# Second mixer of a three-block network: the dense jobs' first piece of work goes into the scan, one gated group per job, centring on ScalarE

## Chip, cores and metric

One core of a Trainium2 chip runs the whole program: three network blocks, one after the other, in float32, at batch 1, 512 tokens and a width of 1024. The metric is the device time of one execution in microseconds. The kernel before took 3704.06 us, the median of three runs (3701.74 to 3704.71).

## What is computed

The change touches the mixer of the second block alone (`second_block` in the reference):

```python
xn = rmsnorm_2(h, mix_norm_w[l])
g_a, g_b, za, z, xbc, dt_raw = jnp.split(xn @ w_in[l], splits, axis=-1)
y_a = gmlp_mixer(za, ...) @ w_proj_a[l]
y_b = mamba2_mixer(z, xbc, dt_raw, ...) @ w_proj_b[l]
merged = sigmoid(g_a + gate_bias[l, 0]) * y_a + sigmoid(g_b + gate_bias[l, 1]) * y_b
h = h + merged @ w_out[l]
# gmlp_mixer: u, v = split(gelu(za)); v in 8 groups of 128 features
v = (vf - mu) * rsqrt(var + EPS_2) * ln_w + ln_b       # per token and group
sv = einsum('gts,bnsgd->bntgd', where(mask, w_s, 0), v) + b_s
return u * sv                                           # per group: "gating"
# mamba2_mixer: conv and silu on xbc, a chunked scan over 32 heads, then
y = (scan + d_skip * xs) * silu(z)                      # 2048 channels
y = yg * rsqrt(mean(yg * yg) + EPS_2) * norm_w          # yg: 4 groups of 512
```

## The kernel before

Each engine has its own program and waits on semaphores for the others; the order on each engine is written out by hand (`tensor`, `scalar`, `vector`, `gpsimd`, `sync` of `SecondMixer`). Activations lie as tiles of 128 channels by 512 tokens. In order of time the second mixer does the following.

**The scan.** 16 pairs of heads. For pair j TensorE turns the channel tile (`turn_pe`, L2375), VectorE makes two scaled copies of it (`factors_dve`, L2815), TensorE forms the chunk states (`states_pe`, L2384), VectorE carries them along (`state_dve`, L2822 and L2827), and TensorE adds up the pair's outputs (`outputs_pe`, L2398 and L2402), which VectorE adds to the skip term (L2683). The weights of the outputs come by another way: SyncE spreads a line of decays over the partitions (L2182) once the outputs of pair j-2 are done, GpSimd subtracts (`relative_pool`, L2483), ScalarE takes two exponentials (`decays_act`, L2602 and L2603), GpSimd (L2493) and VectorE (`aged_dve`, L2838) multiply.

**Tiles between the pairs.** So that TensorE is not idle in the scan, `side_until` lets it work through 30 more tiles of the input projection between those steps: 14 for the scan's own channels, which VectorE convolves (`convolve_dve`, L2797 and L2800) and ScalarE opens (`silu_act`, L2585), and 16 for the gMLP, which ScalarE evicts (`gelu_act`, L2594). A tile is 8 matmuls of 512 columns (weight 2 each, L2229) or 16 of 256 columns (weight 1, L2220), so `TILE` = 16. Each pair has three slots of `SHARE` = 11, after its turn, its states and its outputs. `slot_ends` tells ScalarE and VectorE after which slot they take up which tile. The tiles need 480 of 3 x 16 x 11 = 528, so they end in the slot behind the states of pair 14, and the last four slots are empty.

**The dense jobs.** Then come 28 jobs, each a Strassen step of 28 matmuls of 256 columns per pair of output tiles and 1024 inputs (`Sevens`, L998; the seven products are named 1 to 7 and run in the order 1, 2, 6, 5, 7, 3, 4, four matmuls each). Products 1; 2 and 6; 5 and 7; 3 and 4 share a bank each, so four banks hold a job. GpSimd makes three sums of the weights per slot beforehand (`sums_pool`, L968 to L973); ScalarE copies product 1 (`one_act`, L1024), VectorE takes the rest out (`three_dve` L1029, `five_dve` L1036 and L1038, `all_dve` L1043). A bank may be written again only when the job before has been taken out of it. Jobs 0 to 7 are `ssm_z`, 8 to 11 `gate_a2`, 12 to 15 `w_proj_a`, 16 to 19 `gate_b2`, 20 to 23 `w_proj_b`, 24 to 27 `w_out2`.

**Beside the first jobs.** In jobs 1 to 5 VectorE also normalizes the eight gMLP groups, two per job: centring in four pieces (`normalize_dve`, L2879), gain (L2883) and bias (L2885). TensorE mixes each group over the tokens (`spatial_pe`, L2419), VectorE gates it (`gate_dve`, L2892 and L2896), two groups per job in jobs 2 to 5. Ahead of job 0's eviction VectorE copies the turned mixing weights (`weights_dve`, L2845) and takes the groups' means and variances (`measure_dve`, L2856 to L2863). In jobs 1 to 8 it multiplies two scan tiles by the opened z (`open_dve`, L2752), ScalarE squares them (L2626), and in jobs 4, 6, 8 and 10 VectorE scales four of them (`scale_dve`, L2907) with a root that TensorE summed in jobs 3, 5, 7 and 9 (L2427).

## Time and profile before

| | |
|---|---|
| median of 3 runs | 3704.06 us |
| the profiled execution | 3698.9 us, span 3697.1 us |
| TensorE busy | 3634.8 us (98%) |
| VectorE, GpSimd, ScalarE busy | 1533.4, 1324.0, 757.5 us |
| granted TensorE clock, mean | 0.993 of full |
| chain that ended last | TensorE 94%, VectorE 3%, ScalarE 1%, issue 1%, DMA 1% |

The second mixer lies between about 1622 and 2397 us of the span, its scan between 1710 and 1980. A float32 matmul of the program stands in the trace as two records, so a row with x16 holds 8 matmuls.

### The profile page before, as it was taken

How to read it: one execution, taken by the hardware profiler on the slowest of the kernel's cores; microseconds unless marked ns; L12 is line 12 of the kernel's file. 1: busy time of each engine (PE TensorE's matmuls, PEld its weight loads, DVE VectorE, ACT ScalarE, POOL GpSimd, SP SyncE). 2: the span in 40 equal slices, each digit the busy share in tenths (PEclk: the TensorE clock that was granted, in tenths of full speed). 3: DMA queues.
4: the chain of work that ended last, by engine and by line, in shares of the span. 5: the costliest groups of instructions: out<-in, count | busy, mean ns of one | idle time of the engine just before them, and what ended most of it. 6: DMA issues, size and time to landing. Idle time of an engine off the chain costs nothing.

```text
span 3697.1 us, 44501 instructions
## 1 busy us (share of the span) xinstructions
PE 3634.8 (98%) x18521; PEld 2808.5 (76%) x18521; DVE 1533.4 (41%) x2375; ACT 757.5 (20%) x1354; POOL 1324.0 (36%) x1119
## 2 busy tenths in 40 slices
PE   8999999999999999999999999999999999999999
PEld 7888768775558888864567888888887567758888
DVE  3221210422125422135636632588722464248851
ACT  2000152223211100012332300110012454230000
POOL 4554200000014455414445655456640120016653
PEclk9999999999999999999999999999999999999999
DMA  4322435334132332232232222233223410023222
GB/s 133 91 81 83 87 60 79 58 50 71 55 65 83 88 88 84 83 99 68 86 103 92 78 82 91 80 91 90 79 94 100 80 35 5 6 69 91 81 86 74
DMA packets 370379, 286.22 MB, mean 77 GB/s; under 512 B 11283, under 2 KB 360083, under 8 KB 370180
## 3 DMA queue, kind: packets, MB, share of 16 engines
q1 hardware_dynamic: 369892, 283.11, 28.9%
q8 instruction: 147, 2.41, 0.3%
q14 instruction: 52, 0.43, 0.0%
q10 hardware_dynamic: 288, 0.27, 0.0%
HBM read 280.64 MB, written 2.72 MB: 77 GB/s over the span
## 4 chain that ended last, share of the span: by engine, by line
PE 94%; DVE 3%; ACT 1%; issue 1%; DMA 1%; SPq 0%; DVEq 0%
PE psum L604 42%; PE psum L998 11%; PE psum L1527 7%; PE psum L2229 6%; PE psum L3202 3%; PE psum L1562 2%; PE psum L1322 2%; PE psum L4040 2%; PE psum L2220 2%; PE psum L1318 2%; PE psum L1354 1%; PE psum L3775 1%; PE psum L573 1%; PE psum L3286 1%; PE psum L3306 1%
## 5 line engine op out<-in xcount | busy, mean ns | idle before, releaser
L604 PE MATMUL psum<-work 128*128 128x256 f32 (+1 forms) x2400 | 551.4, 381 | 0.0
L604 PEld LDWEIGHTS psum<-work 128*128 128x128 f32 x2400 | 456.0, 190 | 66.0
L523 POOL TENSOR_TENSOR work<-weight_ring 128x512 f32<-128x512 f32 x132 | 163.4, 1238 | 912.4 <-PE psum L604 731.9
L604 PE MATMUL psum<-work,weight_ring 128*128 128x256 f32 (+1 forms) x2080 | 481.8, 381 | 0.0
L604 PE MATMUL psum<-normalized,weight_ring 128*128 128x256 f32 (+1 forms) x2016 | 468.4, 382 | 2.8 <-DVE normalized L724 2.8
L604 PEld LDWEIGHTS psum<-work,weight_ring 128*128 128x128 f32 x2080 | 395.2, 190 | 57.2
L604 PEld LDWEIGHTS psum<-normalized,weight_ring 128*128 128x128 f32 x2016 | 383.9, 191 | 61.0 <-DVE normalized L724 4.0
L748 DVE TENSOR_TENSOR work<-work,psum 128x512 f32<-128x512 f32 (+1 forms) x100 | 68.7, 687 | 641.8 <-PE psum L604 641.8
L682 ACT ACTIVATE work<-psum 128x256 f32<-128x256 f32 (+1 forms) x100 | 38.6, 386 | 1094.2 <-PE psum L604 1094.2
L2229 PE MATMUL psum<-normalized,weight_ring 128*128 128x512 f32 x512 | 228.4, 598 | 0.0
L785 DVE SCALAR_TENSOR_TENSOR work<-work,vector_columns 128x510 f32<-128x510 f32 (+1 forms) x176 | 223.8, 1330 | 0.0
L998 PE MATMUL psum<-work,weight_ring 128*128 128x256 f32 x896 | 205.9, 379 | 0.0
L1527 PE MATMUL psum<-normalized,weight_ring 128*128 128x512 f32 x448 | 200.2, 596 | 0.0
L998 PE MATMUL psum<-work 128*128 128x256 f32 x832 | 192.6, 379 | 0.0
L998 PEld LDWEIGHTS psum<-work,weight_ring 128*128 128x128 f32 x896 | 170.2, 190 | 23.6 <-issue 0.5
L528 POOL TENSOR_TENSOR work<-weight_ring,work 128x512 f32<-128x512 f32 x132 | 185.7, 1407 | 0.0
L2229 PEld LDWEIGHTS psum<-normalized,weight_ring 128*128 128x128 f32 x512 | 95.1, 191 | 109.4 <-issue 108.3
L1209 POOL TENSOR_TENSOR work<-work 128x512 f32<-128x512 f32 x8 | 10.2, 1270 | 468.1 <-PE psum L1457 271.8
L998 PEld LDWEIGHTS psum<-work 128*128 128x128 f32 x832 | 158.1, 190 | 23.3 <-issue 1.9
L526 POOL TENSOR_TENSOR weight_ring<-weight_ring 128x512 f32<-128x512 f32 x132 | 174.8, 1324 | 0.0
L525 POOL TENSOR_TENSOR work<-work,weight_ring 128x512 f32<-128x512 f32 x132 | 168.3, 1275 | 10.4
L604 PE MATMUL psum<-normalized,work 128*128 128x256 f32 (+1 forms) x672 | 159.9, 381 | 0.0
(538 smaller groups left out, 5328.1 us busy)
## 6 DMA issues: line engine op xcount, KB each, us to landing
weight_ring<-in_w_in SPq DMA_DIRECT2D x73, 1024.0 KB, 7.7
weight_ring<-in_w_ffn_in SPq DMA_DIRECT2D x88, 512.0 KB, 5.1
weight_ring<-in_ffn_w_up SPq DMA_DIRECT2D x44, 512.0 KB, 4.8
weight_ring<-in_ffn_up SPq DMA_DIRECT2D x44, 512.0 KB, 5.2
weight_ring<-in_w_ffn_out SPq DMA_DIRECT2D x16, 1024.0 KB, 5.0
weight_ring<-in_w_out SPq DMA_DIRECT2D x12, 1024.0 KB, 5.0
work<-decay_sums SPq DMA_DIRECT2D x16, 512.0 KB, 4.2
weight_ring<-in_w_proj_b SPq DMA_DIRECT2D x8, 1024.0 KB, 4.9
```

What stands on the lines that cost most here:

```text
L523: own(pool.tensor_tensor(s1, a21, a22, ALU.add))
L525: own(pool.tensor_tensor(s2, s1, a11, ALU.subtract))
L526: pool.tensor_tensor(a21, a11, a21, ALU.subtract)
L528: pool.tensor_tensor(s4, a12, s2, ALU.subtract).then_inc(self.weight_sums.h, 1)
L604: last = pe.matmul(K.ps[:, self.BANK[m] * T:self.BANK[m] * T + self.H], left(m, p), right(pe, m, p), start=first and p == 0, stop=last_par ...
L785: last = dve.scalar_tensor_tensor(out=acc[ct][:, n:T], in0=raw[ct][:, 0:T - n], scalar=weight[ct][n], in1=acc[ct][:, n:T], op0=ALU.mult, o ...
L998: last = pe.matmul(self.half_bank(m), self.left(plan, k, n, m, p), source.right(m, part * pairs + p), start=first and p == 0 and m in (1, ...
L1318: last = pe.matmul(K.bank(b), w, U[:, kt * TM:kt * TM + T], start=kt == 0, stop=kt == KD - 1)
L1322: last = pe.matmul(K.bank(b + h, HALF), w, U[:, at:at + HALF], start=kt == 0, stop=kt == KD - 1)
L1527: last = pe.matmul(K.bank(self.side_bank(place)), plan.slot(k)[:, kt, ct * P:(ct + 1) * P], src[:, kt * stride:kt * stride + T], start=kt ...
L2229: last = pe.matmul(self.bank_of(place), plan.slot(k)[:, kt, ct * P:(ct + 1) * P], src[:, kt * stride:kt * stride + T], start=kt == 0, stop ...
L3202: last = pe.matmul(K.bank(4 + n % 3), plan.slot(k)[:, kt, ct * P:(ct + 1) * P], self.U[:, kt * TM:kt * TM + T], start=kt == 0, stop=kt == ...
```

## The change

- Job 0 runs inside the scan's last slots, behind the last tile. The slots are sized so that tiles and job 0 together fill all 48: `share` spreads 480 + `JOB` (28) evenly, 508 / 48 = 10.6 per slot for 11. Job 0 gets the banks that the tiles leave (1, 2, 0) and bank 7; the groups' sums of squares go to bank 5.
- GpSimd makes the weight sums of slot 0 after pair 13 and not after pair 15. The sums of slot 1 lie in other places, and only the last of the four operations waits for the turned mixing weights. The turning of these waits for the scan's last copies and states, not for its last addition.
- VectorE measures the groups and copies the mixing weights behind job 0's eviction and not ahead of it.
- The centring goes to ScalarE (`normalize_act`: scale by the root, add an offset that VectorE makes once, `offsets_dve`).
- One group is normalized and gated per job, in jobs 1 to 8 and 2 to 9; TensorE mixes one group per job in jobs 2 to 9, after the 22nd matmul.
- Two scan tiles are scaled per job in jobs 6 to 13, for four in jobs 4, 6, 8 and 10. The sums of squares are taken in jobs 3, 5, 9 and 11.
- The sums of the gated tiles (GpSimd, for `w_proj_a`) come one job later.

```diff
@@ SecondMixer.__init__ and places
-        self.dense = Sevens(K, [plans[name] for name in self.DENSE], (0, 1, 2, 5), self.weight_sums_at, self.u_sums + 6 * T, self.made)
+        self.dense = Sevens(K, [plans[name] for name in self.DENSE], (1, 2, 0, 7), self.weight_sums_at, [self.u_sums + 6 * T + i * HALF_BANK for i in range(4)], self.made)
-        self.weight_sums_at = self.bt, self.R
+        self.weight_sums_at = (self.bt, self.bt + T, self.bt + 2 * T), (self.mask, self.acum_n, self.w_rows)
@@ side_pe, share
         for place in range(start, stop):
             yield from self.tile_pe(pe, place)
+        for _ in self.job_pe(pe, "ssm_z", 0):
+            yield 1
...
+    def share(self, slot):
+
+        total = (len(self.tiles) - self.first["xs"] - 2) * TILE + JOB
+        return -(-(slot + 1) * total // (3 * SSM_PAIRS))
@@ tensor
-            self.side_until(side, (3 * j + 1) * SHARE)
+            self.side_until(side, self.share(3 * j))
...
@@ job_pe
-            if name == "ssm_z" and 2 <= c < 6 and at in (3, 19):
-                self.spatial_pe(pe, 2 * c - 4 + (at > 3))
-            if j in (3, 5, 7, 9) and at == 11:
-                self.group_sum_pe(pe, (j - 3) // 2)
+            if 2 <= j < 10 and at == 21:
+                self.spatial_pe(pe, j - 2)
+            if j in self.ROOTS and at == 11:
+                self.group_sum_pe(pe, self.ROOTS.index(j))
+            yield
@@ side_ready_pe
+            if m in (1, 2, 5) and p == 0:
+                bank = {1: 1, 2: 2, 5: 0}[m]
+                pe.wait_ge(*self.was_read(max(place for place in range(len(self.tiles)) if place % 3 == bank)))
@@ turn_weights_pe
-        pe.wait_ge(*S["summed"](SSM_PAIRS))
+        pe.wait_ge(*S["carried"](SSM_PAIRS))
+        pe.wait_ge(*S["stated"](SSM_PAIRS))
@@ gpsimd
-        pool.wait_ge(*S["out"](12))
-        D.sums_pool(pool, 0)
+            if j == 13:
+                pool.wait_ge(*S["out"](12))
+                D.sums_pool(pool, 0)
...
-        pool.wait_ge(*S["turned_w"](1))
-        D.sums_pool(pool, 1)
+        D.sums_pool(pool, 1, lambda: pool.wait_ge(*S["turned_w"](1)))
...
-            if n == self.first_slot["w_proj_a"] - 2:
+            if n == self.first_slot["w_proj_a"] - 1:
@@ scalar, normalize_act
+            if 0 < j <= 8:
+                self.normalize_act(act, j - 1)
...
+    def normalize_act(self, act, g):
+        A, S = self.A, self.s
+        if g == 0:
+            act.wait_ge(*S["offsets"](1))
+        if g > 1:
+            act.wait_ge(*S["mixed"](g - 1))
+        for t in range(NT):
+            n = g + t * GMLP_GROUPS
+            last = act.activation(A(self.vn + (g % 2) * T + t * P, P), A(self.gv + t * D + g * P, P), ACT.Identity,
+                                  scale=A(self.rstd + n, 1), bias=A(self.mv + 2 * n + 1, 1))
+        last.then_inc(S["centred"].h, 1)
@@ vector
-        self.weights_dve(dve, own)
-        self.measure_dve(dve, own)
-        for j in range(8):
+        for j in range(12):
             self.open_dve(dve, j - 1)
             self.scale_dve(dve, j)
...
+            self.dense.three_dve(dve, j, at)
+            if j == 1:
+                self.offsets_dve(dve)
+            if 1 <= j <= 8:
+                self.normalize_dve(dve, own, j - 1)
+            self.five_all_dve(dve, j, at, lambda: self.gate_dve(dve, own, j - 2) if 2 <= j <= 9 else None)
+            if j == 0:
+                self.measure_dve(dve, own)
+                self.weights_dve(dve, own)
@@ scale_dve
-        if j not in (4, 6, 8, 10):
+        if not 6 <= j < 14:
             return
```

**TensorE, last pair of the scan and what follows.** Before: the outputs of pair 14 end, then the turn, the states and the outputs of pair 15, the turning of the mixing weights, job 0.

```order
L2402 MATMUL psum<-work 64x128 x2
L2375 MATMUL psum<-identity,work 128x128 x4
L2384 MATMUL psum<-work 128x128 x3
L2398 MATMUL psum<-work 64x128 x4
L2402 MATMUL psum<-work 64x128 x2
L2398 MATMUL psum<-work 64x128 x2
L2402 MATMUL psum<-work 64x128 x2
L2398 MATMUL psum<-work 64x128 x2
L2402 MATMUL psum<-work 64x128 x2
L2410 MATMUL psum<-identity,work 128x128 x8
L998 MATMUL psum<-normalized,weight_ring 128x256 x8
L998 MATMUL psum<-work 128x256 x8
```

Now, from the last full slot of pair 14 on (L2223 are tiles, L999 is job 0):

```order
L2223 MATMUL psum<-weight_ring,normalized 128x256 x11
L2390 MATMUL psum<-identity,work 128x128 x4
L2223 MATMUL psum<-weight_ring,normalized 128x256 x3
L999 MATMUL psum<-normalized,weight_ring 128x256 x7
L2399 MATMUL psum<-work 128x128 x3
L999 MATMUL psum<-normalized,weight_ring 128x256
L999 MATMUL psum<-work 128x256 x8
L999 MATMUL psum<-normalized,weight_ring 128x256 x2
L2413 MATMUL psum<-work 64x128 x4
```

and behind the outputs of pair 15:

```order
L2417 MATMUL psum<-work 64x128 x2
L999 MATMUL psum<-normalized,weight_ring 128x256 x2
L999 MATMUL psum<-normalized,work 128x256 x4
L999 MATMUL psum<-work,weight_ring 128x256 x4
L2426 MATMUL psum<-identity,work 128x128 x8
L999 MATMUL psum<-normalized,weight_ring 128x256 x8
```

Seven matmuls of job 0 stand ahead of the states, eleven ahead of the outputs and ten behind them; the two ahead of L2413 are the first of product 7.

**VectorE, from the scan's last addition to job 1's eviction.** Before:

```order
L2683 SCALAR_TENSOR_TENSOR work<-work,psum 128x512
L2845 COPY work<-psum 128x512 x2
L2848 MEMSET work 64x8x64
L2856 BN_STATS work<-work 128x6 x32
L2860 BN_AGGR work<-work 128x2 x32
L2863 COPY work<-work 128x32
L1029 TENSOR_TENSOR work<-work,psum 128x2x256
L1036 TENSOR_TENSOR work<-work,psum 128x512
L1038 TENSOR_TENSOR work<-work,psum 128x256
L1043 TENSOR_TENSOR work<-work,psum 128x512
L2752 TENSOR_TENSOR work<-work 128x512 x2
L2879 TENSOR_SCALAR work<-work 128x128 x4
```

Now, from the end of job 0's eviction:

```order
L1044 TENSOR_TENSOR work<-work,psum 128x512
L2892 BN_STATS work<-work 128x6 x32
L2896 BN_AGGR work<-work 128x2 x32
L2899 COPY work<-work 128x32
L2881 COPY work<-psum 128x512 x2
L2884 MEMSET work 64x8x64
L2788 TENSOR_TENSOR work<-work 128x512 x2
L1030 TENSOR_TENSOR work<-work,psum 128x2x256
L2666 SCALAR_TENSOR_TENSOR work<-work 128x32
L2911 TENSOR_TENSOR work<-work 128x512
L2913 TENSOR_TENSOR work<-work 128x512
L1037 TENSOR_TENSOR work<-work,psum 128x512
```

The statistics are behind job 0 and ahead of everything that job 1 needs; the four centrings are gone, and one offset operation stands in their place.

**TensorE, between the outputs of pair 2 and those of pair 3** (turn L2375, states L2384). Before:

```order
L2229 MATMUL psum<-normalized,weight_ring 128x512 x6
L2375 MATMUL psum<-identity,work 128x128 x4
L2229 MATMUL psum<-normalized,weight_ring 128x512 x5
L2384 MATMUL psum<-work 128x128 x3
L2229 MATMUL psum<-normalized,weight_ring 128x512 x6
```

Now:

```order
L2232 MATMUL psum<-normalized,weight_ring 128x512 x5
L2390 MATMUL psum<-identity,work 128x128 x4
L2232 MATMUL psum<-normalized,weight_ring 128x512 x5
L2399 MATMUL psum<-work 128x128 x3
L2232 MATMUL psum<-normalized,weight_ring 128x512 x6
```

With the five ahead of the outputs, 15 tile matmuls now lie between the states of pair 2 and those of pair 3. Between other states there are 16 (one more place with 15 is in the gMLP tiles); before there were 16 and 17 by turns.

## Rows read from the trace of the kernel before

**Rows 1.** Busy time by stretch: start:end, length, engines, PEclk, DMA share, GB/s.
```profile
1950.00:2000.00 50.00, 41.49 (x246) 36.20 (x243) 28.46 (x95) 14.60 (x18) 28.77 (x23) 0.90 0.39 127
2000.00:2050.00 50.00, 49.73 (x252) 43.71 (x250) 45.87 (x71) 13.22 (x18) 27.81 (x20) 1.00 0.21 66
```
**Rows 2.** TensorE's waits, 1620 to 2400 us: total us, times, longest.
```profile
PE psum L2384 <- DVE work L2815: 6.6, 2, 6.2
PE psum L2419 <- DVE work L2892: 6.5, 1, 6.5
```
**Rows 3.** Timeline of TensorE at the scan's end: start, length, x records, [idle before].
```profile
1960.78 0.83 PE L2384 MATMUL psum<-work 128*128 128x128 f32 x6
...
1964.56 0.66 PE L2398 MATMUL psum<-work 128*64 128x128 f32 x8
...
1966.24 0.66 PE L2375 MATMUL psum<-identity,work 128*128 128x128 f32 x4
1973.06 1.65 PE L2384 MATMUL psum<-work 128*128 128x128 f32 x6 [6.16 <-DVE work L2815]
...
1980.28 1.06 PE L2410 MATMUL psum<-identity,work 128*128 128x128 f32 x8 [0.95 <-DVE work L2683]
1981.19 3.62 PE L998 MATMUL psum<-normalized,weight_ring 128*128 128x256 f32 x16
...
1993.28 3.62 PE L998 MATMUL psum<-normalized,weight_ring 128*128 128x256 f32 x16
```
**Rows 4.** Timeline of TensorE in job 5.
```profile
2047.84 1.89 PE L998 MATMUL psum<-normalized,weight_ring 128*128 128x256 f32 x8
2056.23 2.05 PE L2419 MATMUL psum<-work 128*128 128x128 f32 x8 [6.50 <-DVE work L2892]
...
2061.30 1.89 PE L998 MATMUL psum<-work 128*128 128x256 f32 x8
```
**Rows 5.** Timeline of VectorE behind the scan.
```profile
1981.39 1.29 DVE L2845 COPY work<-psum 128x512 f32<-128x512 f32 x2 [1.25 <-PE psum L2410]
...
1983.36 6.29 DVE L2856 BATCH_NORM_STATS2 work<-work 128x6 f32<-128x128 f32 x32
...
1992.05 0.68 DVE L1029 TENSOR_TENSOR work<-work,psum 128x512 f32<-128x512 f32 x1
```
**Rows 6.** Groups of ScalarE by form, 1980 to 2110 us: busy us, mean ns, idle before.
```profile
L2612 ACT ACTIVATE work<-work 128x1024 f32<-128x1024 f32 x8 | 8.5, 1058 | 58.3 <-DVE work L1043 58.3
...
L2539 ACT ACTIVATE work<-work 128x32 f32<-128x32 f32 x1 | 0.3, 324 | 7.3 <-DVE work L2863 7.3
L2541 ACT ACTIVATE work<-work 128x32 f32<-128x32 f32 x1 | 0.2, 233 | 0.0
```
**Rows 7.** Groups of VectorE by form, same stretch.
```profile
L2752 DVE TENSOR_TENSOR work<-work 128x512 f32<-128x512 f32 x16 | 19.0, 1230 | 9.8 <-ACT work L2612 9.8
L2907 DVE SCALAR_TENSOR_TENSOR work<-work,vector_columns 128x512 f32<-128x512 f32 x12 | 15.9, 1385 | 0.0
L2879 DVE TENSOR_SCALAR work<-work 128x128 f32<-128x128 f32 x32 | 13.1, 470 | 0.0
```
**Rows 8.** Line L2752 by itself: shortest, median and longest duration in ns.
```profile
L2752 DVE TENSOR_TENSOR work<-work x16: 684/1390/1759, 1996.5 to 2100.1; 128x512 f32<-128x512 f32 x16
```
**Rows 9.** Timeline of TensorE early in the scan: pair 0, then the states of pairs 2 and 3.
```profile
1712.51 0.68 PE L2375 MATMUL psum<-identity,work 128*128 128x128 f32 x4 [2.28 <-ACT work L2517]
1712.98 7.00 PE L2229 MATMUL psum<-normalized,weight_ring 128*128 128x512 f32 x12
...
1754.78 0.83 PE L2384 MATMUL psum<-work 128*128 128x128 f32 x6
...
1771.57 0.94 PE L2384 MATMUL psum<-work 128*128 128x128 f32 x6
```

**Rows 10.** Timeline of GpSimd behind the scan: the last sum of u.
```profile
1976.01 2.37 POOL L908 TENSOR_TENSOR normalized<-normalized 128x1024 f32<-128x1024 f32 x1
```
**Rows 11.** Busy time by stretch behind the wait of rows 9; PEclk stands third from the end.
```profile
1714.00:1716.00 2.00, 2.00 (x4) 0.84 (x3) 0.18 (x1) 1.98 (x3) 1.08 (x1) 0.50 0.00 0
```

More of the change, by code:

```diff
@@ L934, in part @@
     def part(self, i):
-        return self.K.work[:, self.parts_at + i * self.H:self.parts_at + (i + 1) * self.H]
+        return self.K.work[:, self.parts_at[i]:self.parts_at[i] + self.H]
     def two(self, first, second):
@@ L1028, in three_dve @@
         dve.wait_ge(*self.three(j + 1))
-        dve.tensor_tensor(self.two(c11, self.parts_at + self.H), self.twice(self.part(0)), self.bank(1), ALU.add)\
+        dve.tensor_tensor(self.two(c11, self.parts_at[1]), self.twice(self.part(0)), self.bank(1), ALU.add)\
            .then_inc(self.read_three.h, 1)
@@ L1035, in five_dve @@
         dve.wait_ge(*self.five(j + 1))
-        own(dve.tensor_tensor(self.two(self.parts_at + 2 * self.H, self.parts_at + 3 * self.H), self.twice(self.part(1)), self.bank(2), ALU.add))
+        own(dve.tensor_tensor(self.two(*self.parts_at[2:]), self.twice(self.part(1)), self.bank(2), ALU.add))
         own.wait()
@@ L1055, in residual_dve @@
         dve.wait_ge(*self.read_five(j + 1))
-        own(dve.tensor_tensor(other_half, other_half, self.two(self.parts_at + 2 * H, self.parts_at + 3 * H), ALU.add))
+        own(dve.tensor_tensor(other_half, other_half, self.two(*self.parts_at[2:]), ALU.add))
         dve.tensor_tensor(same_half, same_half, self.two(at, at + H), ALU.add)
@@ L2257, in slot_ends @@
         for n, place in enumerate(range(start, stop)):
-            slot = min(-(-(n + 1) * TILE // SHARE) - 1, 3 * SSM_PAIRS - 1)
+            slot = next(at for at in range(3 * SSM_PAIRS) if self.share(at) >= (n + 1) * TILE)
             out.setdefault(slot, []).append(place)
@@ L2297, in tensor @@
         for name in self.DENSE:
-            for c in range(self.plans[name].groups):
-                self.job_pe(pe, name, c)
+            for c in range(name == "ssm_z", self.plans[name].groups):
+                for _ in self.job_pe(pe, name, c):
+                    pass
     def job_pe(self, pe, name, c):
@@ L2426, in group_sum_pe @@
             pe.wait_ge(*S["groot"](g))
-        pe.matmul(K.bank(7), K.ones[:, :], A(self.gacc + (g % 2) * T, T), start=True, stop=True).then_inc(S["gsummed"].h, 1)
+        pe.matmul(K.bank(5), K.ones[:, :], A(self.gacc + (g % 2) * T, T), start=True, stop=True).then_inc(S["gsummed"].h, 1)
     def gpsimd(self, pool):
@@ L2630, in adds_until, with offsets_dve @@
         return 3 * (t // 4) + t % 4
+    def normalize_act(self, act, g):
[9 more added lines that the diff above has]
+        last.then_inc(S["centred"].h, 1)
+    def offsets_dve(self, dve):
+        A, S = self.A, self.s
+        n = NT * GMLP_GROUPS
+        mean, offset = (A(self.mv, 2 * n)[:, i:2 * n:2] for i in range(2))
+        dve.wait_ge(*S["rooted_v"](1))
+        dve.scalar_tensor_tensor(out=offset, in0=mean, scalar=-1.0, in1=A(self.rstd, n), op0=ALU.mult, op1=ALU.mult)\
+           .then_inc(S["offsets"].h, 1)
     def group_root_act(self, act, own, g):
@@ L2637, in group_root_act @@
             act.wait_ge(*S["scaled"](4 * (g - 1)))
-        own(act.activation(r, K.bank(7), ACT.Ln, scale=1.0 / (4 * P), bias=A(self.eps, 1)))
+        own(act.activation(r, K.bank(5), ACT.Ln, scale=1.0 / (4 * P), bias=A(self.eps, 1)))
         own.wait()
@@ L2871, in normalize_dve @@
         if g == 0:
-            dve.wait_ge(*S["rooted_v"](1))
             dve.wait_ge(*S["spatial_loaded"](16 * 3))
             dve.wait_ge(*S["w_ready"](1))
-        if g > 1:
-            dve.wait_ge(*S["mixed"](g - 1))
-        for t in range(NT):
-            n = g + t * GMLP_GROUPS
-            last = dve.tensor_scalar(A(self.vn + (g % 2) * T + t * P, P), A(self.gv + t * D + g * P, P), A(self.mv + 2 * n, 1),
-                                     A(self.rstd + n, 1), ALU.subtract, ALU.mult)
-        own(last)
-        own.wait()
+        dve.wait_ge(*S["centred"](g + 1))
         own(dve.tensor_tensor(vn, vn, self.every_block(self.gain, g), ALU.mult))
```

52 lines of the change are left out of this document (23 added, 29 removed).

## The prediction

> **What bounds the kernel now.** The page comes first: TensorE is busy for 98% of the span and the chain that ended last runs through it for 94%, so only time in which TensorE waits, or runs below its clock, can be won by a change that removes no matmul. This one removes none. The share of busy time by stretch then tells where such time lies in the second mixer: of 1950 to 2000 us TensorE is busy for 41.49 at a mean clock of 0.90, while in 2000 to 2050 VectorE is busy for 45.87 of 50 [rows 1]. The list of TensorE's waits names two of over six microseconds: 6.2 for the scaled copies of the scan's last pair, and 6.5 for VectorE's gate operation ahead of a spatial mixing [rows 2]. The change aims at both places, so each is priced from TensorE's timeline, and then each engine that it loads is asked what it can hold up instead. Nothing behind the second mixer waits for more than TensorE in order, so a microsecond that is won there comes off the end.
>
> **First part: job 0 in the scan.** From the outputs of pair 14 at 1964.56 to job 0 at 1981.19 TensorE takes 16.63 us [rows 3]. In it lie the outputs of pair 14 (1966.24 - 1964.56 = 1.68), the turn (0.66), the states (0.83, from the earlier pair at full clock), the outputs of pair 15 (1.68) and the turning of the mixing weights (1981.19 - 1980.28 = 0.91): 5.76 us of work. The rest, **10.9 us**, is waiting and half clock (the last states take 1.65 for 0.83). The order now puts 7, 11 and 10 of job 0's matmuls, and the last tile, between these steps. A matmul of a job takes (1993.28 - 1981.19) / 28 = 0.432 us [rows 3], so each cover is 4 to 5 us, over what VectorE needs for the two copies or the state. What released the wait before was a chain that began late: ScalarE took the exponentials of pair 15 only behind the last tile's eviction, and VectorE's multiplication and copies followed. That tile now ends two slots later, so the exponentials are behind the tile before it, and some 17 us of TensorE's work lie between them and their use.
>
> The banks that job 0 takes are those of the last three tiles; the last is read out in 0.6 us and wanted 7 matmuls + states + 5 matmuls = 6.0 us later. GpSimd's weight sums of slot 0, some 5 us, now stand between pairs 13 and 14; pair 14's decays are subtracted later by that, but its exponentials wait in ScalarE's queue for a tile anyway, and nothing of it is wanted for ten microseconds more. I cost it at nothing; without that cover it would be its whole 5 us once.
>
> **Second part: VectorE in jobs 1 to 9.** In job 5 TensorE goes from 2047.84 to 2061.30, 13.46 us, over eight matmuls (3.46) and a mixing (2.05 at half clock, so 1.03) [rows 4]. The rest is **9.0 us** of wait and half clock. It comes from VectorE's load per job. Before, two groups a job: opening 2 x 1.23, centring 8 x 0.47, gain, bias and gate's product 6 x 1.23, gate's addition and eviction 6 x 0.68, and 1.06 for the silu between jobs: 18.7 us [rows 5 to 7], against 28 x 0.432 + 2 x 1.03 = 14.2 for TensorE (gain, bias and product are of the form of L2752 and priced by it). It falls behind by 4.5 us a job over four jobs, and one job gets 4 x 1.385 of scaling besides. Now, in the fullest jobs, 6 to 8: opening 2.46, scaling 2 x 1.385, gain, bias and product 3.69, addition and eviction 5 x 0.68, silu 1.06: 13.4 us against 13.1. Three jobs late by 0.3 us are covered: from product 6 of a job to product 2 of the next but one lie 20 matmuls, 8.6 us. So the wait goes whole.
>
> What ScalarE takes over: an activation of 32 columns takes 0.233, with a bias from memory 0.324 [rows 6], so two such operands add 0.18; a column adds (1058 - 233) / 992 = 0.83 ns; 128 columns come to 0.49 us, a group to 1.97. ScalarE is busy 13.22 of 50 us there [rows 1], so eight groups hide. The Trainium skill speaks against it: "ScalarE: Activation LUTs", Rules for kernel authors, says to use VectorE and not ScalarE for additions and multiplications. The rows make the two equal, 0.49 against 0.47 [rows 7], and what counts is who is waited for. By the rule centring would stay, VectorE's fullest jobs would be 15.3 us, late by 2.2 three times and still covered, and the sum would be 0.3 us better through the first group alone.
>
> **Third part: what it adds.** (a) At the end of job 0 the statistics stand behind the eviction, ahead of all that job 1 needs. From job 0's last matmul VectorE does: last eviction 0.68, statistics 1992.05 - 1983.36 = 8.69, copy and clear 1983.36 - 1981.39 = 1.97 [rows 5], opening 2 x 0.684 [rows 8], eviction 0.68, offsets at most 0.3, then it waits for ScalarE's first centring 1.97, gain and bias 1.37, eviction 1.36: 18.4 us. TensorE asks for that bank at product 5 of job 2: 0.91 + 40 x 0.432 = 18.2. So 0.2 plus the steps between engines: I take **0.5 us** of wait. If the four operations of two SBUF inputs all ran at the longest, 1.759 [rows 8], it would be 4.3 more. GpSimd is idle in most of that stretch, since its next addition waits for ScalarE's square, so I stay at the low end. Ends: 0 and 4.8, with the clock's price below 6.6.
>
> (b) In the scan the slots shrink from 11 to 10.6. From the states of pair 2 to those of pair 3 it took 16.79 us [rows 9], and a chain fills that: state, convolution, silu, exponentials, multiplication, convolution, copies, each behind the other. TensorE's own work there is now 15 x 0.864 + 1.68 + 0.66 + 0.83 = 16.1, with 16 matmuls 17.0. So one pair waits **0.7 us**; the other place with 15 has no convolutions. Ends: 0 and 2, if the pairs with 16 graze it too.
>
> Job 12's wait for the sums of the gated tiles moves one job; they start about 5 us into job 10, take 4 operations like the one of 2.37 us [rows 10], and are wanted 20 us later: nothing.
>
> **Sum:** 10.9 + 9.0 - 0.5 - 0.7 = 18.7 us. The profiled execution took 3698.9, so 3680.2 for it; it is 5.2 below the median of the runs. From the median, **3704.06 - 18.7 = 3685.4 us**.
>
> **The clock.** Behind the wait of 2.28 us twelve records, six matmuls, took 7.00 us for 6 x 0.864 = 5.2 [rows 9]: the granted clock was 0.50 there, the lower of its two levels, 1.2 GHz [rows 11], and a wait of that size costs 1.8 more. Waits below a microsecond show no such trace in the scan.
>
> **Rivals.**
> 1. *VectorE is late in job 2* (a, contended): a wait of 2.3 and 1.8 of clock for the 0.5 of the sum. Gain 15.1, **3689.0 us**. For it: L2752 takes 684 to 1759 ns [rows 8], and the Trainium skill, "GPSIMD Engine Reference", Specifications, has GpSimd share SBUF interfaces with VectorE instructions of two SBUF inputs. Against it: GpSimd's idleness there. Chance 0.12.
> 2. *The fill does not fill*: product 7 stands ahead of pair 15's outputs and waits for GpSimd's last sum of u, which its program puts behind pair 15's multiplication. If these are late, the old wait of 6.2 and 1.8 of clock return in front of the outputs: gain 10.7, **3693.4 us**. Against it: product 7 begins 16 matmuls and the states, 7.7 us, behind the last tile, and the sum takes 2.37 [rows 10]. Chance 0.04.
> 3. *Slower: the scan's chain becomes the bound of every pair.* It decides when the chain is over 18.9 us for the 16.8 seen: then the seven pairs with convolutions wait 2.1 each and drop the clock, 1.8, hence 27 us lost against 19.4 won: **3712 us**. For it: GpSimd's inserted sums and the shifted tiles touch that chain. Against it: the same instructions stand in it, and the inserted sums come after the last convolution. Chance 0.03.
> 4. Several small waits leave the gain below 7.4 us. Chance 0.03.
>
> **Chances.** The forecast holds with 0.78. A measurement of this kernel tells a change of about 0.2%, 7.4 us, from none. Faster by more: 0.78 + 0.12 + 0.04 = 0.94; within: 0.03; slower: 0.03. Range: low, all 19.9 us off a run that is as quick as the profiled one, 3679; high, rival 1 with its upper end (gain 12.6), 3691.5. It leaves out rivals 2 to 4 and the spread of runs: 0.2.
>
> **What would show it.** TensorE's wait list should lose the 6.2 and the 6.5, and show none over a microsecond but the 2.28 of pair 0. Job 0's matmuls should stand in three groups about the states and outputs of pair 15, with the clock at 1.00 from 1960 on. The first states that wait should be those of pair 1 (as before, under 0.5) and pair 3 (0.7). A wait ahead of product 5 of job 2 is the first sign of rival 1; one ahead of product 7 of job 0, of rival 2. VectorE's busy share from jobs 1 to 9 should be even, some 11 of 13 us. The prediction is wrong if TensorE's waits in the second mixer stay above 6 us in all, or if they vanish and the time stays.

## The result and the profile after

| | before | after |
|---|---|---|
| median of the runs timed side by side | 3703.30 us (4 runs, 3701.74 to 3704.71) | 3678.69 us (4 runs, 3677.99 to 3679.58) |
| profiled execution, its span | 3698.9 us, 3697.1 | 3677.99 us, 3676.2 |
| TensorE busy | 98% | 99% |

The ratio is 0.9934, 95% interval 0.9917 to 0.9951, wholly below 1: the change is faster, by less than one per cent. By the medians it gains 24.6 us, by the two profiled executions 20.9; the prediction had said 18.7. Which of these is the change's own is most of what follows.

The page of the changed kernel, busy time and then the chain that ended last:

```profile
PE 3625.2 (99%) x18521; PEld 2799.9 (76%) x18521; DVE 1528.5 (42%) x2344; ACT 771.2 (21%) x1388; POOL 1331.8 (36%) x1119
...
PE 96%; DVE 2%; ACT 1%; DMA 1%; issue 1%; SPq 0%; DVEq 0%; ACTq 0%
```

TensorE holds 96% of the chain instead of 94%. What went is waiting for VectorE. TensorE's waits of the changed kernel, 1620 to 2400 us, beside [rows 2] (total us, times, longest):

```profile
PE psum L2399 <- DVE work L2851: 3.4, 4, 1.3
PE psum L2390 <- ACT work L2533: 2.3, 1, 2.3
```

The 6.2 and the 6.5 are gone. In their place the scan's states wait four times for the scaled copies, 3.4 us in all; that line had 6.6 - 6.2 = 0.4 outside the scan's end before [rows 2]. The busy time by stretch, columns as in [rows 1]:

```profile
1950.00:2000.00 50.00, 50.00 (x286) 43.83 (x285) 27.15 (x98) 16.00 (x23) 21.88 (x20) 1.00 0.38 122
2000.00:2050.00 50.00, 50.00 (x245) 43.70 (x244) 38.36 (x43) 27.15 (x43) 33.81 (x23) 1.00 0.22 69
```

TensorE is busy for all of both stretches at a granted clock of 1.00, where it had 41.49 of 50 at 0.90 in the first [rows 1]. VectorE falls from 45.87 to 38.36 and ScalarE rises from 13.22 to 27.15.

**The scan's end.** TensorE's timeline of the changed kernel, beside [rows 3]:

```profile
1966.75 0.60 PE L2390 MATMUL psum<-identity,work 128*128 128x128 f32 x4
...
1968.48 3.19 PE L999 MATMUL psum<-normalized,weight_ring 128*128 128x256 f32 x14
1971.50 0.83 PE L2399 MATMUL psum<-work 128*128 128x128 f32 x6
1972.17 0.60 PE L999 MATMUL psum<-normalized,weight_ring 128*128 128x256 f32 x2
1972.61 3.62 PE L999 MATMUL psum<-work 128*128 128x256 f32 x16
1976.06 1.03 PE L999 MATMUL psum<-normalized,weight_ring 128*128 128x256 f32 x4
1977.02 0.66 PE L2413 MATMUL psum<-work 128*64 128x128 f32 x8
...
1983.99 3.62 PE L999 MATMUL psum<-normalized,weight_ring 128*128 128x256 f32 x16
```

L2390 turns, L2399 makes the last states, L2413 begins the last outputs, and L999 is job 0, in three groups about them as the order has it. No row carries a wait. Job 1 begins at 1983.99 instead of 1993.28 [rows 3]. The two executions stand 0.06 us apart at pair 0 of the scan (1712.51 [rows 9] and 1712.45), so up to here the change has won 9.29 - 0.06 = 9.2 us.

**Behind job 1.** The chain shows where the two executions stand further on. Of before, first row of the second mixer's input product, then the block behind the mixer, and two long stretches of the third block:

```profile
1634.35 27.66 PE psum L2229 x64
...
2393.83 8.58 PE psum L573 x20
...
2870.38 13.82 PE psum L3202 x32
...
3127.99 23.71 PE psum L3775 x639
```

The same places after:

```profile
1634.28 27.66 PE psum L2232 x64
...
2375.43 8.58 PE psum L573 x20
...
2851.98 13.82 PE psum L3230 x32
...
3106.70 23.71 PE psum L3803 x639
```

From the first to the second row, which I call the mixer's length below, it is 2393.83 - 1634.35 = 759.48 before and 2375.43 - 1634.28 = 741.15 after: 18.3 us. Of these 9.2 were won up to job 1, and the other 9.1 between job 1 and the block behind the mixer, where the wait of 6.5 in job 5 stood. Up to 2851.98 the distance stays 18.40 us; at 3106.70 it is 21.29. The change touches nothing in the third block, and yet that piece takes 254.72 us instead of 257.61.

**VectorE behind the statistics.** VectorE's timeline of the changed kernel, beside [rows 5]: last eviction of job 0, statistics, the two opening operations, the first group's offsets, gain and bias, the eviction that frees the bank of product 5 of job 2, and the next two openings:

```profile
1983.39 0.69 DVE L1044 TENSOR_TENSOR work<-work,psum 128x512 f32<-128x512 f32 x1 [2.05 <-PE psum L999]
1983.99 6.28 DVE L2892 BATCH_NORM_STATS2 work<-work 128x6 f32<-128x128 f32 x32
...
1994.64 1.29 DVE L2788 TENSOR_TENSOR work<-work 128x512 f32<-128x512 f32 x2
...
1996.45 0.19 DVE L2666 SCALAR_TENSOR_TENSOR work<-work 128x32 f32<-128x32 f32 x1
1998.45 0.69 DVE L2911 TENSOR_TENSOR work<-work 128x512 f32<-128x512 f32 x1 [1.81 <-ACT work L2657]
...
2000.50 0.42 DVE L1039 TENSOR_TENSOR work<-work,psum 128x256 f32<-128x256 f32 x1
...
2002.76 3.04 DVE L2788 TENSOR_TENSOR work<-work 128x512 f32<-128x512 f32 x2 [1.12 <-ACT work L2629]
```

From 1983.39 to 2000.92 it is 17.5 us, for 18.4 forecast. TensorE wants the bank 12 matmuls behind 1996.08, at 2001.3, and doesn't wait. ScalarE's centring, as a group of 1980 to 2110 us (busy us, mean ns, idle before):

```profile
L2657 ACT ACTIVATE work<-work 128x128 f32<-128x128 f32 x32 | 13.1, 482 | 2.0 <-DVE work L2666 2.0
```

482 ns, for 0.49 us forecast from two rows of other shapes.

### The profile page after: what moved, and what is told of

It reads as the page before. It is cut to its first block, busy times and chain, and to the rows that moved or that the text cites. A ratio compares the mean times of both kernels' runs of the same rounds, so it can differ in the third digit from the quotient of the medians.

```text
span 3676.2 us, 44506 instructions
## 1 busy us (share of the span) xinstructions
PE 3625.2 (99%) x18521; PEld 2799.9 (76%) x18521; DVE 1528.5 (42%) x2344; ACT 771.2 (21%) x1388; POOL 1331.8 (36%) x1119
## 4 chain that ended last, share of the span: by engine, by line
PE 96%; DVE 2%; ACT 1%; DMA 1%; issue 1%; SPq 0%; DVEq 0%; ACTq 0%
PE psum L604 42%; PE psum L999 13%; PE psum L1529 7%; PE psum L2232 5%; PE psum L3230 3%; PE psum L1564 2%; PE psum L4068 2%; PE psum L1324 2%; PE psum L2223 2%; PE psum L1320 2%; PE psum L1356 2%; PE psum L3803 1%; PE psum L573 1%; PE psum L3314 1%; PE psum L3334 1%; PE psum L1550 1%
## 5 line engine op out<-in xcount | busy, mean ns | idle before, releaser
L999 PE MATMUL psum<-work,weight_ring 128*128 128x256 f32 x896 | 206.0, 379 | 0.0
L999 PE MATMUL psum<-work 128*128 128x256 f32 x832 | 192.6, 379 | 0.0
L999 PEld LDWEIGHTS psum<-work,weight_ring 128*128 128x128 f32 x896 | 170.2, 190 | 23.6 <-issue 0.5
L999 PEld LDWEIGHTS psum<-work 128*128 128x128 f32 x832 | 158.1, 190 | 23.2 <-issue 1.9
```

The costliest lines, as they stand in the source:

```text
L999: last = pe.matmul(self.half_bank(m), self.left(plan, k, n, m, p), source.right(m, part * pairs + p), start=first and p == 0 and m in (1, ...
```

## The experiments

The eleven runs came in three lots. In each, the kernel before ran on the same chip: 3698.82 us (16 runs, 3695.13 to 3704.78) in the first, 3699.97 (21 runs, 3694.68 to 3703.42) in the second, 3700.34 (9 runs, 3693.17 to 3702.18) in the third. Each ratio is against the one of its own lot.

**Both kernels again.** No edit. The profiles are to tell whether the two executions differ outside the second mixer by chance (theory A) or by the change (theory B).

> The kernel before, unchanged, timed and profiled once more. Theory A (the 5.9 us that the change gave over my sum are not of its making: they are in what one execution of the kernel before does to another, outside the second mixer): this profile's span lies nearer to the median of the runs, 3701 rather than 3697, with the difference in the first or third block, and the second mixer's stretches as in the first profile to 0.5 us. Theory B (the change also speeds up something behind the second mixer): the third block takes the same time here as in the first profile of before, and stays 2.5 us longer than in the changed kernel.

> The changed kernel, unchanged, once more. Theory A: mixer 18.4 us shorter as in its first profile, the rest of the span spread by some 2 to 4 us against that profile; ratio 0.9934 within 0.001. Theory B: third block again 2.5 us shorter than in both profiles of before. The wait of the first states of the scan (1.3 us) and the clock behind the wait of 2.28 us: if the clock falls here, the first states do not wait, and the scan is as long.

The kernel before as a second program: 3700.49 us (11 runs, 3695.20 to 3703.80), ratio 1.0002 [0.9993, 1.0010]. The changed kernel: 3679.82 us (5 runs), ratio 0.9948 [0.9935, 0.9960], so 19.0 us.

Neither theory came out whole. The second profile of before spans 3702.0 us, longer than the first as theory A has it, but 2.05 of the 4.9 us lie in the mixer, which A held to 0.5, and the ratio misses A's 0.9934 within 0.001. The third block's piece takes 257.59 us in this profile of before and 254.74 in this one of after, 2.9 apart again, as theory B has it; the later runs, below, weaken B. In the third lot the changed kernel was run once more:

> The changed kernel once more, for the comparison with front_more and with before on the same chip: 19 to 20 us below before (ratio 0.9947), mixer 741.1 us. If the 24.6 us of the first timing were the true gain, 24 to 25 us below before.

3677.46 us (5 runs, 3677.25 to 3682.38), ratio 0.9948 [0.9935, 0.9960]. The medians of this lot stand 22.9 us apart, the means 19.6; in the first lot it was 19.0 and 19.2. Over all the timings beside one another, the first included, the means are 3699.6 us (50 executions) and 3679.6 (14): a gain of 20.0 us, or 0.5%. The first timing's 24.6 came from four executions of before at the upper end of a spread of 11.6 us. The mixer took 761.53 us in the second profile of before, and 741.12 and 741.23 in the two of after.

**The first part taken out** (from the changed kernel): job 0 goes back behind the scan, and a slot gets 11 again.

```diff
-        for _ in self.job_pe(pe, "ssm_z", 0):
-            yield 1
...
-        total = (len(self.tiles) - self.first["xs"] - 2) * TILE + JOB
-        return -(-(slot + 1) * total // (3 * SSM_PAIRS))
+        return 11 * (slot + 1)
...
-            for c in range(name == "ssm_z", self.plans[name].groups):
+            for c in range(self.plans[name].groups):
```

> The changed kernel with job 0 behind the scan again and the old 11 per slot; all else (centring on ScalarE, one group per job, scaling two per job) stays. My sum: only the second part is left, 9.0 us of gain less 0.5, 3694.8 against a before of 3703.3. TensorE's waits at the scan's end come back (6.2, 1.4, 0.9), those of pairs 1 and 3 fall to the 0.4 of before. Rival (the parts need each other, since the measuring of the groups now stands behind job 0 and its cover was made by the fill): a wait in job 2 and a gain under 6.

3688.57 us (6 runs), ratio 0.9970 [0.9958, 0.9983]; mixer 751.12 us. TensorE's timeline of this run, the rows with a wait between 1970 and 2070 us:

```profile
1974.05 1.65 PE L2396 MATMUL psum<-work 128*128 128x128 f32 x6 [6.15 <-DVE work L2848]
...
1977.10 1.12 PE L2410 MATMUL psum<-work 128*64 128x128 f32 x8 [1.41 <-DVE work L2860]
...
2012.32 1.99 PE L999 MATMUL psum<-work 128*128 128x256 f32 x8 [0.43 <-DVE work L1039]
```

The scan's end is as before, 6.15 us of wait and states at half the clock (the six records take 1.65 us for 0.83), and the wait of 6.5 in job 5 is away; a new one of 0.43 stands in job 2. So the second part alone gains 3698.82 - 3688.57 = 10.3 us, for 8.5 expected, and the first part on top of it 3688.57 - 3679.82 = 8.8. The rival, a gain under 6, did not come. In the scan the wait at pair 3 is gone but the one of 1.32 at pair 0 stays: that one is not of the change's making (see below).

**The first part alone** (from the changed kernel): job 0 stays in the scan, while the gating takes two groups per job again, centred on VectorE, in jobs 1 to 5, and the scan's tiles are scaled four at a time in jobs 4, 6, 8 and 10; the sums of squares and of the gated tiles go back to their old jobs as well.

```diff
-            if 2 <= j < 10 and at == 21:
-                self.spatial_pe(pe, j - 2)
+            if name == "ssm_z" and 2 <= c < 6 and at in (3, 19):
+                self.spatial_pe(pe, 2 * c - 4 + (at > 3))
...
+            if 1 <= j <= 4:
+                self.centre_dve(dve, own, 2 * j - 2)
+                self.normalize_dve(dve, own, 2 * j - 2)
...
-        if not 6 <= j < 14:
+        if j not in (4, 6, 8, 10):
...
```

> The changed kernel with the whole of the second part undone: centring on VectorE, two groups per job in jobs 1 to 5, scaling four tiles in jobs 4, 6, 8 and 10; job 0 stays in the scan, and the statistics behind it. My theory: the 9 us of the first part are won, but VectorE, 4.5 us late per job over four jobs, now starts them some 10 us later against TensorE than before (statistics and copies 10.7 us behind job 0's end, where they had lain beside job 0), so the wait of 6.5 us in job 5 grows by about that: waits of 14 to 18 us in jobs 2 to 5, and the time is level with before, 3697 to 3702. Rival (the parts add up): the wait stays 6.5 us and the time is some 9 us below before, 3690.

3701.09 us (11 runs), ratio 1.0007 [0.9998, 1.0015]: nothing is won. TensorE's timeline of this run, its waits over two microseconds behind the scan; L2435 is the spatial mixing:

```profile
2000.09 2.08 PE L2435 MATMUL psum<-work 128*128 128x128 f32 x8 [2.38 <-DVE work L2926]
...
2021.62 2.04 PE L2435 MATMUL psum<-work 128*128 128x128 f32 x8 [5.49 <-DVE work L2933]
...
2059.14 2.04 PE L2435 MATMUL psum<-work 128*128 128x128 f32 x8 [6.04 <-DVE work L2933]
```

The waits at the scan's end are gone here too. But the statistics used to run beside job 0, 12.1 us of TensorE's work, and now they stand behind it. VectorE enters the gating that much later, with the load of two groups a job, and TensorE waits three times, 13.9 us in all, where it waited once for 6.5; 14 to 18 were expected. The mixer's length, parted at the start of job 1, shows both sides of this (us; two profiles of before, three of after):

| | up to job 1 | from job 1 on | mixer |
|---|---|---|---|
| before | 358.93, 361.00 | 400.55, 400.53 | 759.48, 761.53 |
| second part alone | 358.99 | 392.13 | 751.12 |
| first part alone | 349.80 | 413.28 | 763.08 |
| after | 349.71, 349.69, 349.79 | 391.44, 391.43, 391.44 | 741.15, 741.12, 741.23 |

The first part alone returns all that it wins and a little more; it needs the second. The second part doesn't need the first. The first part's price in the forecast's sum, 10.9, holds only with the second part in place; the second's, 9.0, holds within a microsecond without the first (8.4 from job 1 on).

**Centring on VectorE again** (from the changed kernel): four subtractions with a multiplication per group, one group per job, in VectorE's program instead of ScalarE's.

```diff
-                self.normalize_act(act, j - 1)
...
+            if 1 <= j <= 8:
+                self.centre_dve(dve, own, j - 1)
...
+            last = dve.tensor_scalar(A(self.vn + (g % 2) * T + t * P, P), A(self.gv + t * D + g * P, P), A(self.mv + 2 * n, 1),
+                                     A(self.rstd + n, 1), ALU.subtract, ALU.mult)
...
```

> The changed kernel with the centring on VectorE again, one group per job ahead of the first eviction; ScalarE has no part in it and no offset is made. My theory (VectorE's load of 15.3 us in jobs 6 to 8 against 13.1 is covered by the 8.6 us between the release and the use of a bank): no wait of TensorE in jobs 1 to 12 and a time level with the changed kernel within 1 us. Rival (the centring on ScalarE is what frees VectorE): waits of 2 us or more in jobs 6 to 9 and a time 3 to 8 us above the changed kernel.

3680.09 us (5 runs), ratio 0.9946 [0.9933, 0.9960], and the mixer took 741.40 us: level with the changed kernel. TensorE's waits of this run, 1640 to 2410 us:

```profile
PE psum L2390 <- ACT work L2533: 2.3, 1, 2.3
PE psum L2399 <- DVE work L2848: 2.1, 3, 1.3
```

None of them is behind the scan. VectorE's group of these subtractions in this run, 1983 to 2113 us:

```profile
L2909 DVE TENSOR_SCALAR work<-work 128x128 f32<-128x128 f32 x32 | 18.4, 634 | 0.0
```

They take 634 ns for 470 before [rows 7], so 2.5 us a job, and are covered all the same: from job 1 on the mixer takes 391.71 us for 391.44. Moving them to ScalarE gains nothing that can be measured in the time.

**Scaling four tiles at a time, in jobs 6, 8, 10 and 12** (from the changed kernel).

```diff
-        if not 6 <= j < 14:
+        if j not in (6, 8, 10, 12):
...
-        for t in range(2 * j - 12, 2 * j - 10):
+        for t in range(2 * j - 12, 2 * j - 8):
```

> The changed kernel with the scan's tiles scaled four at once in jobs 6, 8, 10 and 12, for two per job in jobs 6 to 13. VectorE's load of job 6 and job 8 rises from 13.4 to 16.2 us and falls in job 7 to 10.6, which the 8.6 us of cover take up: no wait of TensorE in the dense jobs, level with the changed kernel within 1 us. Rival (the spreading of the scaling was needed): a wait in job 7 or 9, 1 to 4 us above the changed kernel.

3678.18 us (5 runs), ratio 0.9946 [0.9933, 0.9958]; mixer 741.13 us. Level as well, and TensorE's waits in the mixer are those of the changed kernel. So neither ScalarE's centring nor the spread scaling carries the gain of the second part; by elimination it is the third piece, one group per job. That is argued: the two were undone one at a time, never both at once.

**The matmuls spread otherwise over the scan** (from the changed kernel). The first 44 slots keep 11 and only the last four get 6; in a second kernel the first 43 also run 4 ahead.

```diff
-        return -(-(slot + 1) * total // (3 * SSM_PAIRS))
+        return 11 * (slot + 1) if slot < 44 else 484 + 6 * (slot - 43)
```

> The changed kernel with 11 per slot up to slot 43, where the tiles end as before, and 6 per slot for job 0 in the last four. If the thinner slots cost what the trace after shows (waits of 1.32, 0.41, 0.40 and 1.25 us in the first four pairs, against 0.40 before), the waits of pairs 2 and 3 go and the time is 1.0 to 1.7 us below the changed kernel, 3677.3. If the last pair's chain (exponentials again behind the last tile) is not covered by 4, 6 and 6 matmuls, a wait of 1 to 3 us stands at the states of pair 15 and the two are level or worse.

3677.51 us (5 runs), for 3677.3 expected, ratio 0.9939 [0.9926, 0.9951]; mixer 739.26 us, 1.9 less than the changed kernel's. The waits of pairs 2 and 3 are gone and no wait stands at the states of pair 15; those of pair 0 (1.32) and pair 1 (0.40) stay, 1.7 us in all, just as in the second profile of before. The second:

```diff
-        return -(-(slot + 1) * total // (3 * SSM_PAIRS))
+        return 11 * (slot + 1) + 4 if slot < 43 else 484 + 6 * (slot - 43)
```

> As front_loaded, with 4 of weight (two matmuls of 512 columns) more in the very first slot, so that the states of pair 0 come 1.7 us of work later, and the tiles end a little earlier. If the first states wait 1.3 us and the next 0.4 only because VectorE's chain is longer than TensorE's work there, both waits go and the time is 1.5 us below front_loaded, 3676.0 where that has 3677.5. If the chain moves with the work, the wait only comes at the next pair: level.

> The kernel of the run front_more once more, beside the changed kernel on the same chip. Its mixer should be 737.6 us where the clock holds behind the 2.28 us wait (738.6 in its first profile, where it fell), against 741.1 for the changed kernel, and its median 3 to 4 us below that of the changed kernel in the same call.

3675.75 us (5 runs), ratio 0.9937 [0.9924, 0.9949]; mixer 738.59 us. Again in the third lot: 3674.09 us (5 runs), ratio 0.9939 [0.9925, 0.9952], mixer 738.72, beside 3677.46 for the changed kernel on the same chip. It is the quickest in both lots that it was in; of its lead of 3.4 us the mixer's length shows 2.5 (741.23 - 738.72), and the intervals of the two ratios overlap. Its ratio is not to be told from that of the first spread (0.9939); only the mixer is 0.5 to 0.7 us shorter, where 1.5 was expected. The 737.6 expected where the clock holds was not tested: behind the 2.28 us at pair 0 the clock fell in both profiles. The scan's waits tell where the changed kernel's time goes. TensorE's timeline of the changed kernel, the rows with a wait up to the states of pair 3:

```profile
1719.55 0.94 PE L2399 MATMUL psum<-work 128*128 128x128 f32 x6 [1.32 <-DVE work L2851]
...
1736.95 0.94 PE L2399 MATMUL psum<-work 128*128 128x128 f32 x6 [0.41 <-DVE work L2851]
...
1754.34 0.94 PE L2399 MATMUL psum<-work 128*128 128x128 f32 x6 [0.40 <-DVE work L2851]
...
1771.72 0.94 PE L2399 MATMUL psum<-work 128*128 128x128 f32 x6 [1.25 <-DVE work L2851]
```

From one pair's states to the next it takes 17.4 us three times here, where the forecast had taken the 16.79 [rows 9] between pairs 2 and 3 for the length of the chain. The difference is in VectorE's timeline; the changed kernel, behind the states of pair 2:

```profile
1755.31 0.29 DVE L2858 COPY work<-psum 128x128 f32<-128x128 f32 x1 [1.03 <-PE psum L2399]
1755.64 0.98 DVE L2863 SCALAR_TENSOR_TENSOR work<-work,psum 128x64 f32<-128x64 f32 x4
1757.03 0.81 DVE L2833 TENSOR_SCALAR work<-psum,vector_columns 128x512 f32<-128x512 f32 x1 [0.41 <-PE psum L2232]
```

The kernel before, the same place:

```profile
1755.98 0.98 DVE L2827 SCALAR_TENSOR_TENSOR work<-work,psum 128x64 f32<-128x64 f32 x4
1756.88 0.81 DVE L2797 TENSOR_SCALAR work<-psum,vector_columns 128x512 f32<-128x512 f32 x1
```

The next convolution now waits 0.41 us for a tile of TensorE's, which ended in time before: with 10.6 instead of 11 per slot two matmuls of that tile come behind the states instead of one, 1.7 us for 0.9. The first spread restores the old slots, and this wait of VectorE's is gone. The second does something else besides. VectorE takes up each tile by the same `share`; with everything 4 ahead this tile counts as ended one slot earlier, so its convolution comes ahead of the copy of the states. VectorE's timeline of the second spread, the same place:

```profile
1754.75 0.81 DVE L2832 TENSOR_SCALAR work<-psum,vector_columns 128x512 f32<-128x512 f32 x1 [2.24 <-PE psum L2232]
...
1757.83 0.28 DVE L2857 COPY work<-psum 128x128 f32<-128x128 f32 x1
```

VectorE now waits 2.24 us for the tile, and TensorE waits for VectorE nowhere: so the matmuls moved ahead of the states are not all that took the waits away; the two were not tested apart. TensorE's waits of the quickest kernel, 1640 to 2410 us, are one row:

```profile
PE psum L2389 <- ACT work L2532: 2.3, 1, 2.3
```

**Eight more matmuls behind the dense jobs** (from the kernel before), work whose output nobody reads, so as to move the third block in time.

```diff
+        for _ in range(8):
+            pe.matmul(K.bank(7, P), K.ident[:, :], K.ident[:, :], start=True, stop=True)
```

> The kernel before with 8 idle transposes (0.9 us at full clock) on TensorE behind the second mixer; they write a bank that nobody reads. The third block took 257.6 us from its first to its last projection stretch in both profiles of before and 254.7 to 255.9 in the changed ones, with the same waits, and a granted clock of 0.83 in 20 us of it before and 1.00 after. If the clock falls or not by the moment at which the same wait comes, this kernel too can show 254.7, though its mixer is that of before. If the gain in the third block is of the change's making, it stays at 257.6.

3699.59 us (8 runs), ratio 0.9999 [0.9989, 1.0010], nothing to tell from before. The added work is not the 0.9 us of the expectation. TensorE's timeline, the added matmuls:

```profile
2390.57 1.95 PE L2301 MATMUL psum<-identity 128*128 128x128 f32 x16
```

Eight such matmuls are 16 records, and what follows starts 1.8 us behind their start. With the waits of 6.2 and 6.5 in place the mixer takes 763.35 us, so 761.6 without them, the length of the second profile of before.

The third block's piece (first row of 32 records of L3202 to the L3775 row, and the same places in the other kernels) took 257.61 and 257.59 us in the two profiles of before and 256.10 here; 254.72, 254.74 and 255.96 in the three of after; 254.73 with the first part alone, whose mixer is no shorter than before's; 254.89, 254.78 and 256.96 with the second part alone, the centring and the scaling undone; 255.95 with the first other spread, 257.85 and 254.87 with the second. One and the same changed program thus shows 254.87 and 257.85, and what it wins in the mixer doesn't decide it. But none of the three profiles without the change lies below 256.10, and the 256.10 here is neither the 254.7 nor the 257.6 of the expectation; that the 2.9 us are chance is likely, not shown. The gain by the means, 20.0 us, leaves little for them beside the mixer's 18.3 to 20.4. What differs in the piece is the clock. The kernel before, 20 us in that piece (columns as in [rows 1]):

```profile
2990.38:3010.38 20.00, 17.10 (x97) 14.90 (x98) 8.74 (x47) 10.93 (x52) 5.33 (x6) 0.83 0.13 47
```

The changed kernel at the same place of the program:

```profile
2971.98:2991.98 20.00, 16.23 (x114) 14.12 (x115) 10.96 (x54) 12.77 (x58) 5.31 (x6) 1.00 0.14 48
```

In both TensorE waits 2.28 us for VectorE; behind that wait TensorE's timeline has matmuls of 256 columns at 1.06 us in the kernel before (3007.64) and at 0.60 in the changed one (2988.11).

## Why the prediction was wrong, and where it was right

**First part, 10.9: right as a mechanism, in size for the execution that it was read from.** The waits (6.2, 1.4 and 0.9) and the half clock at the scan's end went, as the sum had it. Up to job 1 the balance is 9.2, because the new waits of (b) lie in the same piece; with the first other spread, which is without them, it is 358.93 - 347.83 = 11.1. But the half clock is not a fixed price. In the second profile of before the same waits cost 2.2 us more: from the outputs of pair 14 to job 0 it took 17.47 us for 16.63, and job 0 took 13.44 for 12.09.

**Second part, 9.0: right.** From job 1 on 9.1 us against both profiles of before, with no wait for VectorE. Its reason was too wide, though. ScalarE's centring and the spread scaling were counted in the load of 13.4 us a job; either one undone changes nothing in the time, since 20 matmuls cover a deficit that lasts three jobs. The prediction had worked out that cover (15.3 us a job "still covered") and the runs bear it out. By the Trainium skill's rule, which it had cited ("ScalarE: Activation LUTs", Rules for kernel authors), centring belongs on VectorE; here it is worth the same on either (ratios 0.9946 and 0.9948).

**(a), 0.5: rival 1 fell.** VectorE was through after 17.5 us, 0.3 before its bank was wanted. In the stretch behind the statistics the two opening operations took 1.29 together, while GpSimd was idle, as the prediction had argued. GpSimd's timeline, its first addition after that:

```profile
1999.43 1.56 POOL L2488 TENSOR_TENSOR work<-work 128x512 f32<-128x512 f32 x1 [9.01 <-ACT work L2643]
```

At 2002.76, beside GpSimd's sums, the next two openings took 3.04 (mean of the group 1469 ns over 1980 to 2110 us, for 1230 before [rows 7]); there they are covered.

**(b), 0.7: mis-sized.** The states waited four times, 3.4 us. The 1.3 at pair 0 and the 0.4 at pair 1 are not of the change: the second profile of before has both. In the first the 1.3 lay hidden, since the clock had fallen there and twelve records took 7.00 us for 5.32. New are the waits of pairs 2 and 3, 1.7 us, and the first other spread, which takes them away, puts the price at 741.15 - 739.26 = 1.9. That is within the prediction's upper end of 2, but it forecast one wait, at pair 3. The reading that failed is 16.79 us as the chain's length: the chain grew to 17.4 itself, since a tile's end slid further behind the states.

**Rivals 2 and 3** did not come: no wait ahead of product 7 of job 0, and the chain, at 17.4 us, stays below the 18.9 that rival 3 needed.

**The sum against the profile: 18.3 for 18.7, in part by luck.** Among the profiles of before, the one that the sum was read from is the one in which the clock at the scan's end cost least. Against the second the mixer is 20.4 us shorter, and against the kernel with eight more matmuls as much.

**The step that failed is the last one, from the sum to a time: "From the median, 3704.06 - 18.7".** The median of three executions was taken for the level of the kernel before, and "a run that is as quick as the profiled one", 3698.9, for its quick end. The runs show the kernel before between 3693.17 and 3704.78, with a mean of 3699.6 over 50 executions: the start was 4.4 us too high and the low end not low. From 3699.6 the same sum gives 3680.9. Of the 2.2 us that are left to the measured 3678.69, 1.3 are gain that the sum lacks (20.0 by the means for 18.7: the clock at the scan's end was taken at its cheapest, while (b), priced too low, works the other way) and 0.9 the spread of the changed kernel, whose mean is 3679.6. The measured median lies 0.3 below the range, which left the spread of runs out, as the prediction itself says. The 5.2 us by which the profiled execution was quicker than the median was the hint, and it was told and then not used.

**What stays open.** Why the clock falls in one execution and not in the next behind the same wait. Whether the third block's piece is shorter by the change is open too: the eight added matmuls came out at 256.1 us, between 254.7 and 257.6, and don't decide it. One group per job was not tested by itself.

## What to carry to other kernels

Price the parts of a change together: filling one gap moved the start of an engine that was already late, and returned elsewhere all that it had won, until the other part took that lateness away. When filler work is spread thinner, look for the tile boundary that slides over the next thing waited for, and put the filler where the chain beside it is longest. Give the range the spread of the kernel's own executions; three timed runs and a profile that stands 5 us apart from them are a sign that it is wider than the three show. What a clock loss behind a wait costs should be read from more than one execution.

## What the runs showed of the hardware

The granted clock behind one and the same wait differs from execution to execution, and another engine's chain can cancel it. Behind the 2.28 us at pair 0 twelve records of 128x512 took 7.00 us in the first profile of before and 5.32 in the second. TensorE's timeline of the second:

```profile
1715.53 0.63 PE L2375 MATMUL psum<-identity,work 128*128 128x128 f32 x4 [2.28 <-ACT work L2517]
1715.99 5.32 PE L2229 MATMUL psum<-normalized,weight_ring 128*128 128x512 f32 x12
1722.64 0.94 PE L2384 MATMUL psum<-work 128*128 128x128 f32 x6 [1.33 <-DVE work L2815]
```

The 1.7 us that the clock gave were spent, all but 0.2, waiting for VectorE: the states came 7.11 us behind the turn's start here, and 7.31 (1719.82 - 1712.51) there. The changed kernel shows it too: its clock held there in the first profile (5.32) and fell in the third (7.01, and no wait at pair 0's states), and the mixer took 741.15 and 741.23 us. At the scan's end the two executions of before show the reverse; with waits of 6.2, 1.4 and 0.9 in both, the first 16 records of job 0 took 3.62 us in the first [rows 3] and here

```profile
1984.94 4.97 PE L998 MATMUL psum<-normalized,weight_ring 128*128 128x256 f32 x16
```

Here no wait behind took the loss up, and it stayed in the mixer's length.

A change that takes waits away may so take spread away too: the kernel before spans 11.6 us over 50 executions (3693.17 to 3704.78), the changed one 7.2 over 14 (3677.25 to 3684.45). That the waits are the reason is argued from these rows, not shown; with fewer executions a spread also comes out smaller.
